# The addition of the scaled inter-chunk product in an SSD scan, moved from VectorE to GpSimd

## The reference, cut to what matters

```python
def step(h, inp):
    xc, dtc, Bc, Cc = inp
    cum = jnp.cumsum(dtc * A, axis=1)
    seg = jnp.where(causal, cum[:, :, None] - cum[:, None], -jnp.inf)
    wts = jnp.einsum('bign,bjgn->bijg', Cc, Bc)[..., None] * jnp.exp(seg) * dtc[:, None]
    y = jnp.einsum('bijgr,bjgrp->bigrp', wts, xc)
    y = y + jnp.einsum('bign,bgrpn->bigrp', Cc, h) * jnp.exp(cum)[..., None]
    w_end = jnp.exp(cum[:, -1:] - cum) * dtc
    h = h * jnp.exp(cum[:, -1])[..., None, None] + jnp.einsum('bjgn,bjgr,bjgrp->bgrpn', Bc, w_end, xc)
    return h, y
```

## Time and profile before

| | us |
|---|---|
| median of 3 runs | 3533.86 |
| lowest and highest of them | 3529.67, 3542.34 |
| the profiled execution | 3524.27 |
| its span in the trace | 3522.5 |
| PE busy / DVE busy / ACT busy / POOL busy | 3330.8 / 1956.0 / 996.0 / 541.3 |
| mean granted TensorE clock (1 is full speed) | 0.963 |

### The profile page before, as it was taken

One profiled execution on the slowest core, in us unless ns is written; L12 is line 12 of the kernel. 1 busy time (PEld: TensorE's weight loads), 2 busy tenths in 40 slices (PEclk: granted clock), 3 DMA queues, 4 the chain that ended last, 5 costly groups with the idle time before them and its releaser, 6 DMA issues. The chain is left out here.

```text
span 3522.5 us, 47527 instructions
## 1 busy us (share of the span) xinstructions
PE 3330.8 (95%) x18392; PEld 2905.6 (82%) x18392; DVE 1956.0 (56%) x3348; ACT 996.0 (28%) x2021; POOL 541.3 (15%) x551
## 2 busy tenths in 40 slices
PE   7999999998979899999999889999979999999997
PEld 5665665655568899999999878888879999999996
DVE  4995551336767644555445577654455554455546
ACT  2212542434445322112211143322243112211221
POOL 1010100003434211001110002332232011100110
PEclk6999999999989999999999999999989999999998
DMA  5661111133154211111111212222242111111111
GB/s 231 241 263 46 37 51 40 44 83 102 44 197 119 66 40 48 42 42 36 48 42 42 71 36 70 66 66 60 72 128 59 43 37 48 43 45 39 40 48 54
DMA packets 188027, 257.92 MB, mean 73 GB/s; under 512 B 18112, under 2 KB 164040, under 8 KB 182080
## 3 DMA queue, kind: packets, MB, share of 16 engines
q1 hardware_dynamic: 187876, 255.86, 22.1%
HBM read 231.67 MB, written 24.15 MB: 73 GB/s over the span
## 5 line engine op out<-in xcount | busy, mean ns | idle before, releaser
L1867 PE MATMUL PS<-AHL,WH 128*128 128x384 f32 x3072 | 782.7, 335 | 6.0 <-DVE WL L2216 6.0
L1867 PE MATMUL PS<-Y,WH 128*128 128x384 f32 x3072 | 780.0, 334 | 3.1 <-issue 3.1
L2236 DVE SCALAR_TENSOR_TENSOR XT<-PS,MOD,XT 128x384 f32<-128x384 f32 (+2 forms) x1024 | 495.4, 514 | 224.5 <-PE PS L1867 224.2
L1867 PEld LDWEIGHTS PS<-AHL,WH 128*128 128x128 f32 x3072 | 557.2, 189 | 6.6 <-DVE WL L2216 6.6
L1867 PEld LDWEIGHTS PS<-Y,WH 128*128 128x128 f32 x3072 | 554.4, 188 | 4.2 <-issue 3.7
L1867 PE MATMUL PS<-AHL,WL 128*128 128x384 f32 x1536 | 514.7, 335 | 0.0
L1867 PE MATMUL PS<-Y,WL 128*128 128x384 f32 x1536 | 513.1, 334 | 0.0
L2223 DVE TENSOR_TENSOR AHL<-SQ,AHL 128x384 fp32r<-128x384 f32 x192 | 157.2, 819 | 430.3 <-ACT AHL L1972 430.3
L2150 POOL TENSOR_TENSOR SQ<-RT 128x384 f32<-128x384 f32 x192 | 179.8, 937 | 1319.6 <-ACT RT L1967 1300.2
L1961 ACT ACTIVATE WH<-WU 128x1024 fp32r<-128x1024 f32 x128 | 135.5, 1059 | 730.0 <-DMA WU<-in_wff 730.0
L624 PE MATMUL PS<-HT,WR 128*128 128x384 f32 x960 | 324.5, 495 | 12.0 <-PEq L532 7.4
(11 more groups left out here) (361 smaller groups left out, 4480.0 us busy)
## 6 DMA issues: line engine op xcount, KB each, us to landing
WU<-in_wff SPq DMA_DIRECT2D x128, 512.0 KB, 3.6
XT<-in_wmod SPq DMA_DIRECT2D x13, 2048.0 KB, 10.5
F<-in_wmod SPq DMA_DIRECT2D x9, 2048.0 KB, 9.1
OWR<-in_wslots SPq DMA_DIRECT2D x24, 768.0 KB, 5.1
WR<-in_wslots SPq DMA_DIRECT2D x8, 2048.0 KB, 8.2
PW<-in_wslots SPq DMA_DIRECT2D x24, 512.0 KB, 4.5
OWOR<-in_wslots SPq DMA_DIRECT2D x24, 512.0 KB, 4.2
EB<-cum_rows SPq DMA_DIRECT2D x36, 256.0 KB, 4.3
```

The source lines that it names most:

```text
L1867: mm = nc.tensor.matmul(out, wt(w), x, start=(n == 0 and i == 0), stop=(n == len(terms) - 1 and i == 2))
L2236: ins = nc.vector.scalar_tensor_tensor(out=x, in0=PS[:, 3 + j % 4, a - c * TC:e - c * TC], scalar=MOD[:, l, 40 + b, cond:cond + 1], in1=x, ...
```

## The change

VectorE's `inter` keeps the multiplication and loses the addition. GpSimd gets a new function `add_inter(n)`, which is issued last in each round of its loop, behind `carry(n+1)` and `inputs(n+2)`. The waits for the skip term and for `inter_scaled` go with it. It gets two further waits: for `step_taken`, so that it doesn't run against an older `output`, and for its own previous addition. `output` is unchanged.

```diff
@@ shared
+        def y_of_tile(t):
+            return YL[t // 3][:, :, t % 3 * P:(t % 3 + 1) * P]
@@ gpsimd
+                def add_inter(n):
+                    if n in (0, 3):
+                        pool.wait_ge(skip_in[n // 3].sem, skip_in[n // 3].at(16 + 16 * (n // 3)))
+                    if n >= 4:
+                        pool.wait_ge(step_taken.sem, step_taken.at((n - 2) // 2))
+                    if n >= 1:
+                        pool.wait_ge(inter_added.sem, inter_added.at(n))
+                    pool.wait_ge(inter_scaled.sem, inter_scaled.at(n + 1))
+                    y = y_of_tile(steps[n][1])
+                    nc.gpsimd.tensor_tensor(y, y, EB[:, n % 3, :].rearrange("p (q i) -> p q i", q=8), ALU.add).then_inc(inter_added.sem, 1)
+
                 nc.gpsimd.memset(HC[:, :, :], 0.0).then_inc(state_scaled.sem, 1)
                 inputs(0)
                 inputs(1)
                 carry(0)
+                add_inter(0)
                 for n in range(NS):
                     if n + 1 < NS:
                         carry(n + 1)
                     if n + 2 < NS:
                         inputs(n + 2)
+                    if n + 1 < NS:
+                        add_inter(n + 1)
@@ vector
-                def y_of_tile(t):
-                    return YL[t // 3][:, :, t % 3 * P:(t % 3 + 1) * P]
-
                 def inter(n):
                     dve.wait_ge(state_read.sem, state_read.at(n + 1))
                     dve.wait_ge(inter_ready.sem, inter_ready.at(n + 1))
                     e = EB[:, n % 3, :]
                     nc.vector.tensor_tensor(e, e, PS[:, 4:6, :].rearrange("p b n -> p (b n)"), ALU.mult).then_inc(inter_scaled.sem, 1)
-                    if n in (0, 3):
-                        dve.wait_ge(skip_in[n // 3].sem, skip_in[n // 3].at(16 + 16 * (n // 3)))
-                    dve.wait_ge(inter_scaled.sem, inter_scaled.at(n + 1))
-                    y = y_of_tile(steps[n][1])
-                    nc.vector.tensor_tensor(y, y, e.rearrange("p (q i) -> p q i", q=8), ALU.add).then_inc(inter_added.sem, 1)
```

## The result

| | before | changed |
|---|---|---|
| median of the runs | 3535.15 us (4 runs) | 3585.71 us (4 runs) |
| lowest and highest | 3529.67, 3542.34 | 3577.08, 3587.75 |
| span of the profiled execution | 3522.5 us | 3575.3 us |

The ratio is 1.0137, 95% interval 1.0116 to 1.0158: slower by 50.6 us, where 47.4 was forecast. The profiled executions lie 52.8 us apart (3577.08 - 3524.27).

A forecast was written before the change was run, and what follows sets the result against it. TensorE was taken as the bound, waiting for `output` in even steps. A longer wait of 22.8 us plus 24.6 us for the clock gave 47.4 us on a base of 3533.9: 3581 us, range 3553 to 3600.

The forecast's parts named there:

- The bound and the path: Scan: TensorE is the bound; its clearing waits for VectorE's `output` in even steps, seven times, 8.6 us in all.
- The new wait: Even steps: `output` waits for GpSimd's `carry`, `inputs` and addition; 3.08 us later in seven, 1.22 in the eighth, 22.8 us.
- Odd steps: GpSimd and VectorE contend for shared ports, but finish at 864.5, before `carry` at 865.75: no cost, 1.3 us to spare.
- The start: Scan's start: TensorE is held until 801.87 by the load of rows for the exponents, so VectorE's freedom there is worth nothing.
- The freed 28 us of VectorE: VectorE: 18 additions removed, 1.57 us in the row shown; worth nothing in odd steps, and in even ones `output` still waits.
- The clock: Even steps: a fall to 0.50 in each, 5.0 us in seven and 2.1 in the last, less 12.5 now: 24.6 us.
- The eighth step: n = 16, without `inputs`: `output` 1.22 us later, and 2.1 us for the clock.
- The wait alone: Rival: the clock falls as often and as long as now, only the 22.8 us wait counts; 3557 us, chance 0.25.
- GpSimd would be ahead: Rival: from `carry` to `output`, GpSimd's addition is done as early as VectorE's was, and waits vanish; 3511 us, chance 0.04.
- No difference: Rival: later `output` isn't passed on, or fewer clock falls and a short addition offset it; 3541 us, chance 0.06.
- More: Rival: falls last into the update, the addition takes 3.05, odd steps' spare time is used up; 3602 us, chance 0.07.
- Rival 2: Faster, 3511 us: GpSimd's addition is early, or the count of `inter_added` no longer holds `output`; chance 0.04.

The follow-up runs named there:

- The first experiment: Changed kernel with GpSimd's addition issued ahead of `inputs` (carry, addition, inputs): 3562.7 us, ratio 1.0088.
- the fourth: Changed kernel with GpSimd's `inputs` issued twice in each round, a dose of 1.86 us more ahead of the addition: 3585.33 us, ratio 1.0157.
- the third: Changed kernel with `output` waiting only for additions up to the previous step, the old wait kept at n = 10: 3509.66 us, ratio 0.9941.
- sixth: Changed kernel with `output` waiting only for additions up to the previous step in all even steps; GpSimd's addition 11 waits for `output`: 3504.04 us, ratio 0.9912.
- the two filled kernels: Changed kernel and kernel before, TensorE doing 17 and 4 unused dense products in even-step waits: 3531.69 us (ratio 1.0008) and 3510.73 us (0.9939).
- the last experiment: Changed kernel with the addition back on VectorE in the rounds that have an `output`, GpSimd keeping the other ten: 3531.55 us, ratio 0.9999.
- seventh: Kernel before with VectorE doing `output` ahead of its own addition, with the weaker count, nothing moved to GpSimd: 3501.87 us, ratio 0.9905.
- second experiment: Changed kernel with TensorE doing 17 unused dense float32 products before its wait for `step_taken` in even steps: 3531.69 us, ratio 1.0008.

## Why the prediction was right

**The bound and the path.** `output` in even steps was on TensorE's path, and its start decided. The first experiment moved it by the queue in front of it, the fourth by a dose, the third and sixth took the wait away; each time the clearing's wait came out within 0.2 us of the forecast.

**The new wait.** 3.08 us later was forecast, and the wait grew by 3.06. The duration of the addition, drawn from two rows of other sizes, was 2.35 and is 2.34. The row nearest in size, 1.90, would have been wrong. As a check with the clock out of the way: the two filled kernels differ by 3531.69 - 3510.73 = 21 us (24 by the ratios), for a forecast of 22.8.

**What was costed at nothing.** Odd steps: the last experiment has them at nothing within 0.15%. There was more spare time than the 1.3 us of the prediction at full clock, 1.75 us. The start: TensorE was held for 7.4 us by the row load (6.7 before). The freed 28 us of VectorE: nothing, by the sixth and seventh experiments.

**The clock.** A fall in every step was forecast and came. Its size was the term that was off: 5.0 us per step forecast, 6.6 measured in seven distances. The prediction ended each low stretch with the read. Each went on into the exponents behind it where it lasted 14 us, and through the update, up to the next chunk, in the four of 17 us. Net of what the clock took before, that is 33.5 us in the traces for 24.6. The eighth step, for which the sum has 1.2 and 2.1 us, gave almost nothing in the end: the stretch from the last even multiplication to the end of the program is only 0.3 us longer. The runs with the gaps filled give the same parts once more. By the ratios the fill is worth 46 us in the changed kernel and 22 in the kernel before, 24 net, and the wait 24; by the medians 54, 23, 31 and 21. That the parts add up to the whole is no check, since each is a difference of the same four kernels. By the ratios both terms are close to the forecast, by the medians and the traces the clock's is 7 to 9 us too small. The intervals of the ratios, 5 to 7 us to each side, leave this open, and that the total came within 3 us is in part luck.

**The rivals.** The wait alone, 3557, is out: the clock took the larger share. That GpSimd would be ahead is out: it took 6.17 us for its three operations where at most 3.1 would have done. "No difference" is out by the interval. "More", 3602, had one part right: four of seven falls reach through the update. Rival 2's time of 3511 was reached when `output` stopped waiting for the addition, the second way to it that the prediction names. The Trainium skill's exclusive lock ("SBUF — State Buffer", Who interferes with whom) fits the odd step, where operations of 1.90, 2.34 and 1.2 us last 2.88, 3.35 and 2.4, at no cost to the end.

## What to carry to other kernels

Before work is moved from a busy engine to an idle one, ask who waits for its result and what stands in front of it in the new queue; 15% busy doesn't mean that the engine is free at that moment. A wait for a count can ask for more than the data needs: here the reader of one tile waited for additions to another, and putting the awaited operation first was worth 0.9%, where the choice of engine was worth nothing that the runs can tell. And cost a wait of TensorE together with the clock that follows, by the work that will stand at the low level and not as a fixed price per microsecond of waiting.

## What the runs showed of the hardware that was not expected

- Waits of TensorE of 1.2 us, once in some 21 to 24 us of work without a gap, were followed by a granted clock of 0.50 in four of seven cases in one kernel and six of seven in another; waits of 2.45 us were in each of seven. Filling 0.9 of the 1.23 us with dense products removed the falls in all seven distances.
- The low level lasted 6.8 us in each fall of the kernel before, and 10 to 17 us in the changed kernel, with the same work behind the wait. What sets its length isn't shown.
- A wait of 6.33 us cost the program no more than one of 4.29 that the runs can tell: the fall came some 2.5 us before the work, and 11.0 us of work stood at the low level instead of 14.5.
- Work at the low level cost 0.45 to 0.46 us more for each us that it lasted, in four kernels with different waits.
- A GpSimd multiplication whose second input is broadcast takes 1.90 us for 128x1024, an addition with two full inputs 2.34.
- The spread of a kernel's runs can itself be a sign: in the kernel before it is 25 us and goes with the mean granted clock, from 0.965 to 0.957. It isn't a clean one. Versions without falls in the seven distances spread by 5 to 10 us in six runs, but by 14 in ten (second experiment), and the first experiment, with a fall behind every wait, by 3.5 in four.
